# The last down-projection with the activations stationary and 512 weight columns moving, and the closing norm with tokens on partitions

## The reference, cut to what matters

```python
def rms_norm_2(x, g):
    xf = x.astype(jnp.float32)
    y = xf * lax.rsqrt(jnp.mean(xf * xf, axis=-1, keepdims=True) + EPS)
    return (y * g.astype(jnp.float32)).astype(x.dtype)
...
        x = x + m @ w_out[l]

        h2 = rms_norm_2(x, norm2_g[l])
        x = x + jnp.square(jax.nn.relu(h2 @ mlp_w1[l])) @ mlp_w2[l]
    return rms_norm_2(x, final_g)
```

## Time and profile before

| | us |
|---|---|
| median of 3 runs | 1788.87 |
| the runs | 1788.28, 1788.87, 1791.19 |
| span of the profiled execution (first to last instruction) | 1788.0 |
| its PE busy | 1717.7 (96%) |
| its DVE busy | 1295.5 (72%) |
| its ACT busy | 992.0 (55%) |
| mean granted TensorE clock | 0.979 of full speed |

### The profile page before, as it was taken

The page is one execution under the profiler, slowest core; times in us unless marked ns, Lnnn a source line. Parts: engine busy times, 40 slices in busy tenths (PEclk is TensorE's granted clock), DMA queues, the critical chain, the costliest instruction groups (busy, mean ns, idle before and its releaser), DMA issues.

```text
span 1788.0 us, 38474 instructions
## 1 busy us (share of the span) xinstructions
PE 1717.7 (96%) x14874; PEld 1609.7 (90%) x14874; DVE 1295.5 (72%) x2130; ACT 992.0 (55%) x1543; POOL 2.5 (0%) x8
## 2 busy tenths in 40 slices
PE   7999899999999999998999999989999999889998
PEld 6999899899999989998988999989999998789997
DVE  6777767657777887777767777777787775567776
ACT  5445555445444564445555444568878875344443
POOL 0000000000000000000000000000000000000000
PEclk9999999899999999999999999999999999999999
DMA  6555443115555455554425565445555540145553
GB/s 233 187 177 189 140 140 107 60 49 180 184 181 188 154 165 179 187 186 136 148 79 175 188 188 177 159 159 181 175 188 178 177 154 4 63 130 183 184 184 118
DMA packets 75721, 277.74 MB, mean 155 GB/s; under 512 B 8416, under 2 KB 8672, under 8 KB 75104
## 3 DMA queue, kind: packets, MB, share of 16 engines
q1 hardware_dynamic: 75168, 273.58, 47.5%
q0 software_dynamic: 448, 2.62, 0.4%
HBM read 274.07 MB, written 2.10 MB: 154 GB/s over the span
## 4 chain that ended last, share of the span: by engine, by line
PE 89%; DVE 6%; ACT 3%; issue 1%; DMA 0%; DVEq 0%; SPq 0%; ACTq 0%
PE ps L461 87%; DVE w_lo L450 1%; PE ps L2270 1%; ACT w_hi L442 1%; DVE rstd L566 0%; DVE arena L634 0%; ACT arena L1938 0%; DVE rstd L624 0%; DVE h L533 0%; DMA x<-x_t 0%; DVE x L787 0%; DVE arena L757 0%; DVE arena L761 0%; ACT h L525 0%; DVE a_lo L777 0%
## 5 line engine op out<-in xcount | busy, mean ns | idle before, releaser
L461 PE MATMUL ps<-h,w_hi 128*128 128x256 f32 (+1 forms) x3460 | 756.2, 309 | 0.0
L450 DVE TENSOR_TENSOR w_lo<-raw,w_hi 128x1024 fp32r<-128x1024 f32 x514 | 623.3, 1214 | 104.6 <-ACT w_hi L442 95.2
L442 ACT ACTIVATE w_hi<-raw 128x1024 fp32r<-128x1024 f32 x514 | 538.8, 1050 | 235.6 <-PE ps L461 220.6
L461 PE MATMUL ps<-h,w_lo 128*128 128x256 f32 x2066 | 598.0, 290 | 28.5 <-DVE h L630 14.3
L461 PEld LDWEIGHTS ps<-h,w_hi 128*128 128x128 f32 x3460 | 572.4, 195 | 29.5
L461 PEld LDWEIGHTS ps<-h,w_lo 128*128 128x128 f32 x2066 | 401.9, 195 | 35.2 <-issue 21.4
L461 PE MATMUL ps<-h_of_feed_forward,w_hi 128*128 128x512 f32 (+1 forms) x1008 | 340.5, 383 | 0.0
L461 PE MATMUL ps<-a_hi,w_lo 128*128 128x256 f32 x1032 | 293.6, 285 | 8.8 <-DVE a_lo L777 8.8
L461 PE MATMUL ps<-a_hi,w_hi 128*128 128x256 f32 x1032 | 292.3, 283 | 0.0
L461 PE MATMUL ps<-a_lo,w_hi 128*128 128x256 f32 x1032 | 292.3, 283 | 0.0
L461 PE MATMUL ps<-h_of_feed_forward,w_lo 128*128 128x256 f32 x960 | 269.9, 283 | 0.6 <-issue 0.6
(11 more groups left out here) (327 smaller groups left out, 1226.0 us busy)
## 6 DMA issues: line engine op xcount, KB each, us to landing
raw<-weights SPq DMA_DIRECT2D x514, 512.0 KB, 3.4
con<-shape_constants SPq DMA_DIRECT2D x1, 1618.0 KB, 10.4
x<-x_t SPq DMA_DIRECT2D x1, 1024.0 KB, 4.9
stored<-x POOLq DMA_DIRECT2D x1, 1024.0 KB, 5.0
x<-stored POOLq DMA_DIRECT2D x1, 1024.0 KB, 7.9
out_t<-arena SPq DMA_DIRECT2D x4, 256.0 KB, 2.1
arena<-p_t POOLq DMA_DIRECT2D x2, 256.0 KB, 4.6
par<-parameters SPq DMA_DIRECT2D x1, 172.5 KB, 2.4
```

Of the source, the lines that this page charges most:

```text
L442: A.activation(w_hi[:, u % RING, 0:n], raw[:, u % RING, 0:n], ACT.Copy).then_inc(s_hi, 1)
L450: V.tensor_tensor(w_lo[:, u % RING, 0:n], raw[:, u % RING, 0:n], f(w_hi[:, u % RING, 0:n]), SUB)\
L461: return TE.matmul(o, lhsT, rhs, start=start, stop=stop, skip_group_check=True)
```

## The change

In the last stage, `mlp`, alone:

- The down-projection is turned round. The stationary operand is now 128 tokens of `a`, and 512 columns of the weight unit move (`tokens_down`). Bank q of PSUM holds token block q // 2 and half q % 2 of the 1024 output features. Per unit there are 4 banks x 3 = 12 matmuls of 512 columns, where there were 24 of 256.
- `x` is added by PE: after the norm's sums at the opening, 16 fp32 products with `x` tiles (128 features by 128 tokens) stationary and the identity moving put `x`, transposed, into banks 0 to 3 (`residual`). The four additions of DVE at the end are gone, and with them the new `x`.
- The last tiles run in another order: up(31) comes ahead of down(29) (its unit comes one place earlier in the stream), and down(30) and down(31) are both done for token block 0 first, then for block 1 (`last_tokens_down`), and each finished bank is signalled (`s_bank`).
- The closing norm has the tokens on partitions, so that its sum runs along the free dimension: ACT squares a bank with an accumulating output, DVE adds the two sums of a block (128 x 1), ACT takes the root (128 x 1), DVE the reciprocal (128 x 1), DVE multiplies bank by factor and gain (128 x 512). Bank 2 goes another way: DVE multiplies by the gain early, ACT by the factor. The gain, 512 KB with a copy for each partition, is loaded by POOL's queue once `x` of the MLP is there.
- The output is stored as `[2, 128, 1024]`, four pieces of 256 KB.

```diff
@@ ffn_units @@
+    if not gated:
+        out[-4], out[-3] = out[-3], out[-4]
@@ build @@
+        def final_act(act):
+            A.activation(root_of[:, 2 * len(stages):2 * len(stages) + 1], ones[:, 0:1], ACT.Sqrt)
+            def squares(q):
+                act.wait_ge(s_bank, q + 1)
+                A.activation(normed[:, q, :], ps[:, q, :], ACT.Square, accum_out=bank_sum[:, q:q + 1]).then_inc(s_bsq, 1)
+            def root(b):
+                act.wait_ge(s_bsum, b + 1)
+                A.activation(block_root[:, b:b + 1], block_sum[:, b:b + 1], ACT.Sqrt, bias=eps_col, scale=1.0 / D).then_inc(s_bsd, 1)
+            squares(0)
+            squares(1)
+            root(0)
+            squares(2)
+            squares(3)
+            root(1)
+            act.wait_ge(s_bg, 1)
+            act.wait_ge(s_brs, 2)
+            A.activation(normed[:, 2, :], gained, ACT.Copy, scale=block_rstd[:, 1:2]).then_inc(s_fin, 1)
+        def final_dve(dve):
...
+            def summed(b):
+                dve.wait_ge(s_bsq, 2 * b + 2)
+                V.tensor_tensor(block_sum[:, b:b + 1], bank_sum[:, 2 * b:2 * b + 1], bank_sum[:, 2 * b + 1:2 * b + 2], ADD)\
+                    .then_inc(s_bsum, 1)
...
+            dve.wait_ge(s_gain, 16)
+            summed(0)
+            inverse(0)
+            scaled(0)
+            scaled(1)
+            dve.wait_ge(s_bsq, 3)
+            V.tensor_tensor(gained, ps[:, 2, :], gain_of(2), MUL).then_inc(s_bg, 1)
+            summed(1)
+            inverse(1)
+            scaled(3)
@@ Ffn @@
             def up(self, j):
+                if not self.gated and j == self.n - 1:
+                    return self.u0 + 2 * self.n - 4
             def down(self, j):
+                if not self.gated and j == self.n - 3:
+                    return self.u0 + 2 * self.n - 3
@@ ffn_pe @@
+            def residual():
+                for q in range(4):
+                    for k in range(4):
+                        mm(ps[:, q, k * P:k * P + P], x[:, q % 2 * 4 + k, q // 2 * P:q // 2 * P + P], ident, k == 0, False)
+            def tokens_down(u, j, q, stop):
+                b_, c_ = slice(q // 2 * P, q // 2 * P + P), slice(q % 2 * 512, q % 2 * 512 + 512)
+                l_hi, l_lo = a_hi[:, j % f_.bufs, b_], a_lo[:, j % f_.bufs, b_]
+                return mm3(ps[:, q, :], l_hi, l_lo, w_hi[:, u % RING, c_], w_lo[:, u % RING, c_], False, stop)
+            def last_tokens_down():
+                for b in range(2):
+                    for j in (f_.n - 2, f_.n - 1):
+                        if b == 0:
+                            pe.wait_ge(s_act, count(f_, j, None))
+                            pe.wait_ge(s_lo, nth(f_.down(j)))
+                        for q in (2 * b, 2 * b + 1):
+                            last = tokens_down(f_.down(j), j, q, j == f_.n - 1)
+                            if j == f_.n - 1:
+                                last.then_inc(s_bank, 1)
...
                 norm_pe(pe, f_.norm)
+                if not f_.gated:
+                    residual()
...
-                if j >= 1:
+                if f_.gated:
+                    down(j - 1, i)
+                elif j == f_.n - 1:
+                    down(j - 2, i)
+                    last_tokens_down()
+                elif j < f_.n - 2:
                     down(j - 1, i)
@@ sync @@
-            for p_ in range(4):
-                sp.wait_ge(s_nrm, nrm_at[len(stages)] + p_ + 1)
-                sp.dma_start(out[:, pair_of(p_), :], whole[:, pair_of(p_), :]).then_inc(s_out, 16)
+            for n_ in range(2):
+                sp.wait_ge(s_nrm, nrm_at[len(stages)] + n_ + 1)
+                store(n_)
+            sp.wait_ge(s_fin, 1)
+            store(2)
+            sp.wait_ge(s_nrm, nrm_at[len(stages)] + 3)
+            store(3)
@@ gpsimd @@
+            pool.wait_ge(s_x, 4 * order["mlp"])
+            pool.dma_start(gain, a_gain).then_inc(s_gain, 16)
@@ tensor @@
-            norm_pe(pe, len(stages))
```

More of the change, by code:

```diff
@@ L135, in parameter_columns @@
     put("norm2", columns(a["norm2_g_2"][0]))
-    put("final", columns(a["final_g_2"]))
     put("q_a", columns(a["mla_q_a_norm"][0]))
@@ L393, in build @@
         order = {s: n for n, s in enumerate(stages)}
-        late = [s[:3] in ("ffn", "ple", "mlp") for s in stages] + [False]
+        late = [s[:3] in ("ffn", "ple", "mlp") for s in stages]
         sq_at, nrm_at = [0], [0]
@@ L635, in norm_dve @@
                 last.then_inc(s_nrm, 1)
-                if p_ and n < len(stages):
+                if p_:
                     rest(p_ - 1)
-            if n < len(stages):
-                rest(3)
-                dve_split(dve, unit_base[stages[n]] + 2)
+            rest(3)
+            dve_split(dve, unit_base[stages[n]] + 2)
+        gain = arena[:, 12288:12288 + D]
+        gained = arena[:, 13824:13824 + 512]
+        normed = arena[:, 14336:14336 + 4 * 512].rearrange("p (q n) -> p q n", q=4)
@@ new lines, in final_dve, with gain_of, inverse, scaled @@
+        def final_dve(dve):
+            def gain_of(q):
+                return gain[:, q % 2 * 512:q % 2 * 512 + 512]
+            def summed(b):
+                dve.wait_ge(s_bsq, 2 * b + 2)
+                V.tensor_tensor(block_sum[:, b:b + 1], bank_sum[:, 2 * b:2 * b + 1], bank_sum[:, 2 * b + 1:2 * b + 2], ADD)\
+                    .then_inc(s_bsum, 1)
+            def inverse(b):
+                dve.wait_ge(s_bsd, b + 1)
+                V.reciprocal(block_rstd[:, b:b + 1], block_root[:, b:b + 1]).then_inc(s_brs, 1)
+            def scaled(q):
+                dve.wait_ge(s_bsq, q + 1)
+                dve.wait_ge(s_brs, q // 2 + 1)
+                V.scalar_tensor_tensor(normed[:, q, :], ps[:, q, :], block_rstd[:, q // 2:q // 2 + 1], gain_of(q), MUL, MUL)\
+                    .then_inc(s_nrm, 1)
+            dve.wait_ge(s_gain, 16)
[8 more added lines that the diff above has]
+            scaled(3)
@@ L700, in down @@
                 pe.wait_ge(s_lo, nth(u, i))
+                if not f_.gated:
+                    for q in range(4):
+                        last = tokens_down(u, j, q, False)
+                    last.then_inc(s_prod, 1)
+                    return
                 for m in range(KT):
@@ L3248 @@
         "shape_constants": shape_constants(),
+        "final_gain": np.tile(a["final_g_2"].reshape(1, D), (P, 1)),
     }
```

25 lines of the change are left out of this document (15 added, 10 removed).

## The result

The changed kernel takes 1774.91 us (median of 4 executions: 1773.71, 1774.46, 1775.37, 1779.68) against 1788.57 for the kernel before (4 executions, 1786.67 to 1791.19): a ratio of 0.9924, 95% interval 0.9904 to 0.9943, 13.7 us less.

What follows compares the result with a forecast made beforehand. The prediction took PE's matmuls, 87% of the span, as the bound. Pitch -3.4, opening -1.4, stall +0.4 and tail -5.85 gave -10.2 us from 1788.0, so 1777.8, plus 0.87 for the median: 1778.6 us, range 1776.0 to 1782.0.

Steps and rivals of the forecast that it cites:

- The pitch, -3.4: MLP down-projection: 12 matmuls at 0.230 us take 2.76 us, 0.11 less per unit, over 31 units -3.4 us.
- The opening, -1.4: MLP opening: identity products hide in PE's wait, the clock stays at 1.00, down(0) falls from 4.29 to 2.87 us.
- The stall, +0.4: End of PE's work: PE waits 0.5 us for tile 31's `a`, behind ACT's last weight split, 0.4 more than before.
- The tail, -5.85: Closing norm and stores: 6.0 us behind the last streamed column in place of 11.85, -5.85 us.
- the 0.2 for two stores at once: End of the tail: the two last stores share the DMA engines, adding perhaps 0.2 us.
- The sum: Whole kernel: -3.4 - 1.4 + 0.4 - 5.85 = -10.2 us against the profiled span of 1788.0, giving 1777.8.
- The 0.87: Whole time: the median of the runs lies 0.87 us above the span, so 1777.8 becomes 1778.6.
- The range: Whole time: 1776.0 to 1782.0 us, the low end allowing half a microsecond of spread.
- The opening gives something: Rival at the MLP opening: it gives nothing, -1.4 becomes about 0, 1780.0 us; chance 0.13.
- the width saves something: Rival in the down-projection: 512 columns take 0.240 us, twice 256, so -3.4 becomes 0, 1782.0 us; chance 0.10.
- the closing is shorter by more than forecast: Rival at the end: the closing is no shorter, -5.85 and -1.4 become 0, 1785.9 us; chance 0.04.
- a change of bank restarts nothing: Rival in the down-projection: each bank change restarts the stream, 0.11 us each, 14 us added, 1792.7 us; chance 0.02.

Runs made afterwards that it cites:

- after_shift: Changed kernel with 8 unused parameter columns reserved, so all tiles behind them lie where they lay before; ratio 0.9937 against the kernel before.
- after_256: Changed kernel with every 512-column down-projection matmul cut into two of 256, tokens still stationary; MLP 194.31 us against the changed kernel's 191.85.
- both experiments: Kernel before with the 16 identity products added (down(0) 2.97 us, 1782.57 us whole); changed kernel without them (down(0) 5.07 us, 1776.41 us whole).
- after: The changed kernel itself, against the kernel before: 1774.91 us, ratio 0.9924.

## Why the prediction was right, and where it was wrong

*What bounds it, and that it gets faster:* right. PE's own work is the bound, no new wait took the place of those removed, and PE waits nowhere for a weight split inside the loop.

*The pitch, -3.4:* measured -2.9. The down-projection itself gave more, 2.743 us per unit, 0.229 a matmul, and 0.129 less in place of the 0.11; the term says "The up-projections, 16 matmuls each, stay", and they didn't: 2.808 became 2.844, by the tile's new place and the wide matmuls together, as `after_shift` (2.798) and `after_256` (2.805) show. With the old place (`after_shift`) the term is 31 x 0.137 and 30 x 0.010, -4.5.

*The opening, -1.4:* right, and shown to be the identity products' effect on the clock by both experiments. Against the other profiles of the old form, with up to 5.29 us for down(0), it is worth up to 2.4. The products ran at 0.112 us per record, 3.6 us in all, under the 4.1 that I took as the most.

*The stall, +0.4:* +0.5, with the wait of 0.57 against a forecast of 0.5, and for the reason told.

*The tail, -5.85:* -6.3, the largest term. It is read from the rows alone; no run puts the old closing norm back. The steps came in the order of the forecast. What was over-sized is the root, 0.29 us for one column against the 0.39 taken from a row of 128 x 8, the sum and the reciprocal at 0.15 and 0.16 against 0.18, and the 0.2 for two stores at once.

*The sum:* the MLP became 10.0 us shorter against 10.2 forecast. That the sum came out so close is partly luck, since errors met: the work itself gave 11.7 (201.87 to the 190.20 of `after_shift`), and the new place of the tile took 1.65 back.

*The step that failed* is the one behind the sum, "against the profiled span of 1788.0: 1777.8. The median of the runs lies 0.87 above the span, so 1778.6". It puts everything ahead of the MLP at no change, without a reason, and it takes one profiled execution for the kernel. Ahead of the MLP there was no change in the instructions, and yet:
- The gated loops became 0.8 us shorter, 0.4 in each of two, because a parameter list that got eight columns shorter moved a tile that PE streams from. That is shown by the runs that put the tile elsewhere.
- The part ahead of the MLP was 1586.1 us in the one profile that the sum starts from and 1580.1 in the first one after, 6.0 less, and lay between 1578.7 and 1588.3 over 18 profiles, in large part with the clock. By this spread the other 5.2 us can be chance. That they are isn't shown: the seven profiles with the new place of the tile average 3 us less than the five with the old one.
- The baseline had a down(0) of 4.29 us, the shortest of six, so the opening was worth up to 1 us more to other executions.
- The 0.87 mixed two executions. The profiled one after took 1773.71 with a span of 1771.92, and all four have the same 1.8 us around the span; so the span of 1788.0 belongs to an execution of about 1789.8, 1.2 above the median. This cost little: from the median of 1788.57 the sum of -10.2 gives 1778.4.

The pooled difference is 11.4 us by means and 12.3 by medians, and the MLP (-10.0 to -11.2, by the two profiles of each kernel) with the gated loops (-0.8) makes 10.8 to 12.0. The rest of the 13.7 is within what a draw of four and four executions gives with a spread of 3.9 us. The range had half a microsecond for that spread and should have had two or three.

*The rivals.* The opening gives something, the width saves something (`after_256`), the closing is shorter by more than forecast, and a change of bank restarts nothing: a unit with four changes has 12 matmuls in 2.74 us, with no start more than 0.24 behind the one before.

## What to carry to other kernels

A wait of PE can cost twice, once as itself and again as half clock in what follows it. Here 4.7 us of wait did (down(0) took 4.29 to 5.29 us in place of 2.9), and waits of 1.16 and 0.57 us did not: the clock behind them was 1.00. Independent matmuls that are put into the wait, even useless ones, get the second part back. A forecast of a term is only as good as the baseline that it is set against: take it as a difference, and give the range the spread that several executions of the same kernel show (3.9 us here), above all where the clock falls in stages that the change doesn't touch. And when a buffer gets narrower, everything behind it moves: compare the period of a loop that the change leaves alone before calling it unchanged.

## What the runs showed of the hardware that I had not expected

The pitch of the same matmuls depends on where the moving tile lies in SBUF: 8.467, 8.487, 8.433, 8.513 and 8.520 us per tile of the gated loops at five addresses 32 bytes apart, in rising order, one per cent from the shortest to the longest, the same to the last digit wherever one was run again or reached by another edit. What reads the tile in these loops is PE, as the moving operand. At one of the places the pitch also depends on the matmuls ahead: the up-projection of the MLP takes 2.844 us behind matmuls of 512 columns and 2.805 behind matmuls of 256 (`after`, `after_256`).

A matmul that also loads its weights costs 0.119 us at 256 columns and 0.229 at 512, at a granted clock of 1.00.

An execution's time varied with a standard deviation of 3.9 us over 82 executions. In the traces much of that goes with short stages in which the granted clock falls in one execution and not in the other, and one stretch of small stages took 114.3 to 118.5 us, 116.80 and 114.34 in two executions that both had 1.00 there.
